# Which engine forms the low halves of 26 weight chunks: the mixer's convolution and narrow projections

## The chip, the cores and the metric

The kernel runs on one core of one Trainium2 chip. The metric is the device time in microseconds, the median over runs. A profiled execution carries the record of every engine: TensorE (PE, with its weight loads as PEld), VectorE (DVE), ScalarE (ACT), GpSimd (POOL) and SyncE (SP, which issues DMAs). Numbers such as L2278 are lines of the kernel.

## The reference

Two transformer blocks in float32 over 512 tokens of width 1024. The part that the change touches is the input projection of the first block's mixer, once for the 512 tokens (`mix_sublayer`) and once for the 256 tokens of a context sequence (`context_states`):

```
h = modulate(rms_norm(x, norm_pre), mod3[:, 0], mod3[:, 1])
u_f, z, xbc, dt_raw = split(h @ w_in, ...)        # 256, 768, 1792, 24 columns
xbc = silu(centred_dwconv(xbc, conv_w) + conv_b)
dt  = softplus(dt_raw + dt_bias)
...
h = modulate(rms_norm(ctx, norm_pre), ...)        # 256 context tokens
xb, dt_raw = split(h @ w_in[:, 1536:], ...)       # 1280, 24 columns
xb = silu(centred_dwconv(xb, conv_w[:, 512:]) + conv_b[512:])
dt = softplus(dt_raw + dt_bias)
```

A scan over states, a Fourier mixing, an output projection, a feed-forward layer and a whole second block follow.

## The kernel before, in words

Every large product is made with three TensorE passes in a reduced type. Each operand is held as a high half (its value rounded to that type) and a low half (value minus high half), and PE adds high x high, high x low and low x high (L1486 to L1488). Activations are split where they are made; weights are split as they arrive.

The weights come as one stream of chunks of up to 128 x 1024 numbers in the order in which PE uses them. For chunk j:

- SP loads it into one of three `raw` buffers. It waits until both halves of chunk j - 3 have been formed, which frees the buffer (`load`).
- ACT writes the high half into one of three `whi` buffers (L1837), when the load has landed and PE is through with chunk j - 3.
- DVE or GpSimd writes the low half, `raw - whi`, into one of three `wlo` buffers. DVE does it in one subtraction over the chunk (L2278), GpSimd in two over half the chunk each (L2776 and L2777). Both wait for the high half. PE waits for the low half when it begins the chunk.

The split of chunk c + 2 is placed at the step `begin` of chunk c, in each engine's program order. All engines run their own parts of one list of steps, in its order, so an operation that waits holds up all that is behind it on its engine.

Which engine forms the low half is decided by the name that a chunk carries in the stream: names in the tuple `LOW_BY_VECTOR` (L666) go to DVE, the first six chunks too, all others to GpSimd. `split` in `number` counts the events, and both engines' `w_low` follow that count. GpSimd does nothing else but one multiplication in each rotary embedding of the second block.

The steps around the change, in order of time:

- `ffn1c` (until 595 us): feed-forward layer over the context, low halves by DVE.
- `dt` (one chunk of 24 columns) and `xbc` (14 chunks, N = 512). For each output tile ACT evacuates PSUM with the middle tap of the convolution (L1916), DVE adds the outer taps (L2345, L2346, which read PSUM), ACT applies Silu (L2041), and six of the tiles are transposed by PE (L1567) one chunk later and copied by ACT (L2025). The rest of the context's feed-forward is woven between: DVE adds the norm's result (L2461, L2464), ACT squares (L1976), DVE sums the squares (L2431), PE reduces them over partitions (L1529), and then the pre-norm of the context is made in eight rounds that go from DVE (L2446) to ACT (L2000) and back to DVE (L2267), with two buffers. Then softplus (L2241 to L2257) and small products over `dt` (L1578).
- `cdt` (one chunk) and `cxb` (10 chunks, N = 256): the same for the context. Woven between are its softplus: DVE L2241, L2242, ACT L2047, DVE L2244, ACT L2049, DVE L2251 to L2257, L2488. Behind it PE makes twelve small products (L1598), ACT their exponentials (L2060), each in the engines' order.
- `uf`, `z`, `wo`: the other projections, with the scan beside them. Their low halves are formed by DVE before and after. From 921 us on GpSimd forms the low halves again.

PSUM has eight banks, six of which are handed round in turn to output tiles and small products.

Of the kernel before, what the change touches and what calls it, by code (L numbers as in the profile page):

```python
# [662 lines left out]
LN_EXP = "natural_log_exp_and_others"  # L663


LOW_BY_VECTOR = ("ffn1c", "dt", "xbc", "cdt", "cxb", "uf", "z", "wo")  # L666


SIGNALS = {
# [24 lines left out]
def number(S, stream):  # L694
# [3 lines left out]
    def mark(*event):  # L698
        sem = SEM_OF[event[0]]
        count[sem] = count.get(sem, 0) + 1  # L700
        assert event not in at, event
        at[event] = count[sem]
# [15 lines left out]
    def split(j):  # L718
        mark("hi", j)
        mark("lov" if stream[j][0] in LOW_BY_VECTOR or j < 2 * NS else "lop", j)  # L720

# [2139 lines left out]
```

## Time and profile before

| | |
|---|---|
| median of 3 runs | 3460.84 us (3460.06 to 3464.72) |
| the profiled execution | 3463.49 us, of which the span of the records is 3462.2 us |
| PE busy | 3381.9 us, 98% |
| DVE busy | 1610.9 us, 47% |
| ACT busy | 1418.3 us, 41% |
| GpSimd busy | 1321.3 us, 38% |
| granted TensorE clock, mean | 0.994 |
| chain that ended last | PE 87%, DVE 5%, ACT 3%, issue 2%, DMA 2%, POOL 1% |

Of the 40 slices of the span, GpSimd is idle in the six from about 433 to 910 us; in these the low halves are DVE's. The busy times say which engine has room. Whether a wait costs anything is seen in the waits of PE and in the chain that ended last, read for the stretch in question. A "duration" of DVE or GpSimd in these records runs from the start of the instruction and holds any time for which it is held up inside.

### The profile page before, as it was taken

How to read it: one execution, taken by the hardware profiler on the slowest of the kernel's cores; microseconds unless marked ns; L12 is line 12 of the kernel's file. 1: busy time of each engine (PE TensorE's matmuls, PEld its weight loads, DVE VectorE, ACT ScalarE, POOL GpSimd, SP SyncE). 2: the span in 40 equal slices, each digit the busy share in tenths (PEclk: the TensorE clock that was granted, in tenths of full speed). 3: DMA queues.
4: the chain of work that ended last, by engine and by line, in shares of the span. 5: the costliest groups of instructions: out<-in, count | busy, mean ns of one | idle time of the engine just before them, and what ended most of it. 6: DMA issues, size and time to landing. Idle time of an engine off the chain costs nothing.

```text
span 3462.2 us, 44383 instructions
## 1 busy us (share of the span) xinstructions
PE 3381.9 (98%) x16880; PEld 2716.5 (78%) x16880; DVE 1610.9 (47%) x3080; ACT 1418.3 (41%) x2397; POOL 1321.3 (38%) x1032
## 2 busy tenths in 40 slices
PE   7999999998999999999999999999999999999998
PEld 5888899885688887777776888887877776788887
DVE  6856566666520115755542343232865452344142
ACT  4223455654532224354443344343354453344242
POOL 2776200000044443434433444444534333444443
PEclk9999999999999999999999999999999999999999
DMA  7566455221123323223222222323323222223332
GB/s 305 201 217 218 128 185 170 87 88 49 49 91 92 104 86 103 89 68 98 80 91 73 91 92 89 101 89 115 100 74 95 79 75 92 91 80 96 99 96 87
DMA packets 117716, 373.26 MB, mean 108 GB/s; under 512 B 15360, under 2 KB 16256, under 8 KB 117120
## 3 DMA queue, kind: packets, MB, share of 16 engines
q1 hardware_dynamic: 115024, 364.74, 32.5%
q10 hardware_dynamic: 2480, 5.68, 0.5%
q8 instruction: 135, 2.21, 0.3%
q14 instruction: 77, 0.63, 0.1%
HBM read 356.73 MB, written 2.10 MB: 104 GB/s over the span
## 4 chain that ended last, share of the span: by engine, by line
PE 87%; DVE 5%; ACT 3%; issue 2%; DMA 2%; POOL 1%; SPq 1%; ACTq 0%; DVEq 0%; POOLq 0%
PE ps L1486 26%; PE ps L1488 25%; PE ps L1487 25%; PE ps L1756 2%; PE ps L1773 1%; PE ps L1738 1%; PE ps L1529 1%; ACT b L1837 1%; DVE b L2278 1%; PE ps L1733 1%; DVE b L2446 1%; PE ps L1546 1%; PE ps L1797 1%; PE ps L1808 1%; DMA b<-b 1%
## 5 line engine op out<-in xcount | busy, mean ns | idle before, releaser
L1486 PE MATMUL ps<-b,b 128*128 128x512 f32 (+1 forms) x4688 | 1768.5, 377 | 27.3 <-DVE b L2267 6.0
L1488 PE MATMUL ps<-b,b 128*128 128x512 f32 (+1 forms) x4688 | 1733.9, 370 | 0.0
L1487 PE MATMUL ps<-b,b 128*128 128x512 f32 (+1 forms) x4688 | 1732.5, 370 | 0.0
L2776 POOL TENSOR_TENSOR b<-b,b 128x512 fp32r<-128x512 f32 (+1 forms) x494 | 629.1, 1273 | 2082.3 <-ACT b L1837 2078.8
L1486 PEld LDWEIGHTS ps<-b,b 128*128 128x128 f32 x4688 | 883.9, 189 | 216.0 <-issue 52.2
L1488 PEld LDWEIGHTS ps<-b,b 128*128 128x128 f32 x4688 | 883.6, 188 | 153.7
L1487 PEld LDWEIGHTS ps<-b,b 128*128 128x128 f32 x4688 | 884.6, 189 | 148.5 <-issue 5.5
L1837 ACT ACTIVATE b<-b 128x1024 fp32r<-128x1024 f32 (+1 forms) x618 | 603.8, 978 | 318.7 <-PE ps L1488 306.5
L2777 POOL TENSOR_TENSOR b<-b,b 128x512 fp32r<-128x512 f32 (+1 forms) x494 | 650.0, 1316 | 0.0
L1901 ACT ACTIVATE b<-b 128x512 fp32r<-128x512 f32 (+1 forms) x110 | 64.8, 589 | 347.7 <-DVE b L2322 244.7
L2408 DVE CUSTOM_DVE_ANT_0 b<-b,b,b 128x1024 bf16<-128x1024 f32 x108 | 188.2, 1742 | 39.7 <-DMA b<-in_ada 32.2
L2313 DVE SCALAR_TENSOR_TENSOR b<-ps,b,b 128x511 f32<-128x511 f32 x88 | 66.0, 750 | 248.7 <-ACT b L1891 248.7
L2278 DVE TENSOR_TENSOR b<-b,b 128x1024 fp32r<-128x1024 f32 (+2 forms) x124 | 138.9, 1123 | 81.1 <-ACT b L1837 80.7
L2322 DVE TENSOR_TENSOR b<-ps,b 128x512 f32<-128x512 f32 (+1 forms) x66 | 39.6, 599 | 277.4 <-PE ps L1488 271.1
L2659 DVE CUSTOM_DVE_ANT_0 b<-ps,b 128x128 f32<-128x128 f32 (+2 forms) x192 | 87.2, 454 | 157.9 <-PE ps L1756 131.3
L2154 ACT ACTIVATE b<-b,b 128x128 f32<-128x128 f32 (+2 forms) x192 | 102.2, 534 | 97.0 <-DVE b L2666 68.7
L1976 ACT ACTIVATE b<-b 128x512 f32<-128x512 f32 (+1 forms) x112 | 64.2, 582 | 186.3 <-DVE b L2341 60.1
L2170 ACT ACTIVATE b<-ps 128x128 f32<-128x128 f32 (+2 forms) x192 | 69.0, 409 | 150.6 <-PE ps L1756 150.2
L1891 ACT ACTIVATE b<-ps,b 128x512 f32<-128x512 f32 x88 | 68.6, 779 | 97.1 <-PE ps L1488 96.8
L2336 DVE TENSOR_TENSOR b<-b,ps 128x512 f32<-128x512 f32 x32 | 22.0, 687 | 185.3 <-PE ps L1488 185.3
L2328 DVE TENSOR_TENSOR b<-b,b 128x512 fp32r<-128x512 f32 (+1 forms) x110 | 70.2, 638 | 80.8 <-ACT b L1901 80.8
L2677 DVE TENSOR_SCALAR b<-b,b 128x128 f32<-128x128 f32 (+2 forms) x192 | 100.9, 526 | 6.8
(240 smaller groups left out, 2378.6 us busy)
## 6 DMA issues: line engine op xcount, KB each, us to landing
b<-in_w SPq DMA_DIRECT2D x454, 512.0 KB, 3.4
b<-in_ada SPq DMA_DIRECT2D x86, 512.0 KB, 5.6
b<-in_w SPq DMA_DIRECT2D x80, 384.0 KB, 3.1
b<-in_w SPq DMA_DIRECT2D x80, 320.0 KB, 2.9
b<-b SPq DMA_DIRECT2D x160, 64.0 KB, 2.0
b<-in_const SPq DMA_DIRECT2D x24, 256.0 KB, 3.8
b<-in_x SPq DMA_DIRECT2D x2, 1024.0 KB, 11.3
out<-b SPq DMA_DIRECT2D x8, 256.0 KB, 2.0
```

What stands on the lines that cost most here:

```text
L1486: pe.matmul(out, a[0], b[0], start=first, stop=False, **kw)
L1487: pe.matmul(out, a[0], b[1], start=False, stop=False, **kw)
L1488: return pe.matmul(out, a[1], b[0], start=False, stop=last, **kw)
L1837: act.activation(whi[j % NS][:, 0:nk * w], raw[j % NR][:, 0:nk * w], ACT.Copy).then_inc(up("hi", j), 1)
L2154: m = act.activation(q[:, 0:hi - lo], q[:, 0:hi - lo], ACT.Exp, bias=sx[:, 1:2], accum_out=sx[:, 2:3])
L2278: dve.tensor_tensor(wlo[j % NS][:, 0:nk * w], raw[j % NR][:, 0:nk * w], whi[j % NS][:, 0:nk * w].bitcast(F32), ALU.subtract).then_inc(up(" ...
L2328: dve.tensor_tensor(hl[:, i % 11, 0:N], q[:, 0:N], hh[:, i % 11, 0:N].bitcast(F32), ALU.subtract).then_inc(up("hl", f, i), 1)
L2408: m = dve.tensor_tensor_reduce(spare[:, :], ada_slot(x)[:, :], cb[:, w, :], 1.0, pv("ada_b", p), ALU.mult, ALU.add, mod[:, p, w:w + 1])
L2659: dve.tensor_tensor_reduce(Lg[u % 6][:, 0:w], PB[st["bank"][p]][:, 0:w], mk, 0.125, -3e38, ALU.add, ALU.max, sx[:, 0:1]).then_inc(up("t1", ...
L2677: dve.tensor_scalar(q, q, sx[:, 4:5], None, ALU.mult).then_inc(up("pr", a, l, u), 1)
L2776: pool.tensor_tensor(wlo[j % NS][:, 0:h], raw[j % NR][:, 0:h], whi[j % NS][:, 0:h].bitcast(F32), ALU.subtract)
L2777: then(pool.tensor_tensor(wlo[j % NS][:, h:2 * h], raw[j % NR][:, h:2 * h], whi[j % NS][:, h:2 * h].bitcast(F32), ALU.subtract), "lop", j)
```

## The change

Four names leave the tuple, so that GpSimd forms the low halves of the chunks that carry them: `dt` (1), `xbc` (14), `cdt` (1) and `cxb` (10). GpSimd's two subtractions take the place of DVE's one for each. Nothing else changes: the loads, the high halves, the order of steps and the buffers are the same.

```
-LOW_BY_VECTOR = ("ffn1c", "dt", "xbc", "cdt", "cxb", "uf", "z", "wo")
+LOW_BY_VECTOR = ("ffn1c", "uf", "z", "wo")
```

## Rows read from the trace of the kernel before

**Rows 1.** Page, part 1: busy time, share of the span, instructions.
```profile
PE 3381.9 (98%) x16880; PEld 2716.5 (78%) x16880; DVE 1610.9 (47%) x3080; ACT 1418.3 (41%) x2397; POOL 1321.3 (38%) x1032
```

**Rows 2.** Windows: stretch, length, busy of each engine, granted clock, DMA share, GB/s.
```profile
700.00:720.00 20.00, 16.73 (x123) 16.32 (x122) 11.51 (x27) 14.77 (x27) 0.00 (x0) 0.83 0.41 132
```

**Rows 3.** Waits of PE, 592 to 745 us: total, times, longest.
```profile
PE ps L1486 <- DVE b L2346: 2.2, 1, 2.2
...
PE ps L1598 <- DVE b L2488: 1.0, 1, 1.0
```

**Rows 4.** Line L2278, 592 to 729 us: durations in ns, first and last start.
```profile
L2278 DVE TENSOR_TENSOR b<-b,b x26: 350/1216/1226, 592.8 to 725.1; 128x1024 fp32r<-128x1024 f32 x24, 128x192 fp32r<-128x192 f32 x2
```

**Rows 5.** Timeline, start and duration: one chunk's halves with DVE quiet.
```profile
925.46 1.05 ACT L1837 ACTIVATE b<-b 128x1024 fp32r<-128x1024 f32 x1
...
926.65 1.30 POOL L2776 TENSOR_TENSOR b<-b,b 128x512 fp32r<-128x512 f32 x1 [2.90 <-ACT b L1837]
927.90 1.29 POOL L2777 TENSOR_TENSOR b<-b,b 128x512 fp32r<-128x512 f32 x1
```

**Rows 6.** Timeline: another pre-norm of N = 256, with GpSimd at work.
```profile
356.53 0.98 POOL L2776 TENSOR_TENSOR b<-b,b 128x320 fp32r<-128x320 f32 x1 [0.44 <-ACT b L1837]
356.81 0.98 DVE L2446 SCALAR_TENSOR_TENSOR b<-b,b,b 128x256 f32<-128x256 f32 x1
357.47 1.06 POOL L2777 TENSOR_TENSOR b<-b,b 128x320 fp32r<-128x320 f32 x1
357.71 1.09 DVE L2267 SCALAR_TENSOR_TENSOR b<-b,b,b 128x256 fp32r<-128x256 f32 x1
...
361.05 0.48 DVE L2446 SCALAR_TENSOR_TENSOR b<-b,b,b 128x256 f32<-128x256 f32 x1
```

**Rows 7.** Timeline: a one-input DVE operation beside GpSimd and alone.
```profile
1494.46 1.30 POOL L2777 TENSOR_TENSOR b<-b,b 128x512 fp32r<-128x512 f32 x1
1494.49 1.48 DVE L2677 TENSOR_SCALAR b<-b,b 128x384 f32<-128x384 f32 x1
...
1496.09 0.42 DVE L2677 TENSOR_SCALAR b<-b,b 128x384 f32<-128x384 f32 x1
```

**Rows 8.** Timeline: the last sum of squares of the context's norm.
```profile
635.69 1.05 ACT L1837 ACTIVATE b<-b 128x1024 fp32r<-128x1024 f32 x1
637.93 0.71 ACT L1976 ACTIVATE b<-b 128x256 f32<-128x256 f32 x2
638.41 0.42 DVE L2431 TENSOR_TENSOR b<-b,b 128x256 f32<-128x256 f32 x1
638.88 0.70 PE L1529 MATMUL ps<-b,b 128*128 128x256 f32 x2 [1.19 <-DVE b L2431]
```

**Rows 9.** Timeline: three chunks with the context's pre-norm beside them.
```profile
655.61 0.77 ACT L1916 ACTIVATE b<-ps,b 128x512 f32<-128x512 f32 x1
...
668.87 0.77 ACT L1916 ACTIVATE b<-ps,b 128x512 f32<-128x512 f32 x1
...
671.24 0.63 ACT L2041 ACTIVATE b<-b 128x512 f32<-128x512 f32 x1 [0.65 <-DVE b L2346]
...
672.23 0.60 PE L1567 MATMUL ps<-b,b 128*128 128x128 f32 x4
```

**Rows 10.** Timeline: the high half of a context chunk.
```profile
704.57 1.06 ACT L1837 ACTIVATE b<-b 128x1024 fp32r<-128x1024 f32 x1
```

**Rows 11.** The chain that ended last, in order of time: start, duration, what.
```profile
705.78 1.13 DVE b L2278
...
707.31 0.22 DVE b L2252
...
708.77 0.28 DVE b L2488 x2
...
713.93 0.58 PE ps L1486
```

**Rows 12.** Windows, columns as in rows 2.
```profile
711.60:718.40 6.80, 4.58 (x22) 4.47 (x22) 2.25 (x4) 3.87 (x10) 0.00 (x0) 0.50 0.47 157
```

## The prediction, made before the changed kernel was built

> **What bounds the kernel now.** I read the page first, then the waits of PE and the chain that ended last over the stretch where the 26 chunks are split, and then the timelines of DVE, ACT and GpSimd side by side there. PE is busy for 98% of the span [rows 1], so a microsecond taken from DVE or given to GpSimd counts only where PE waits for it. From 592 to 745 us PE waits little: 1.19 us for the last sum of squares (L2431) [rows 8], 1.0 us for the end of the context's softplus (L2488), 2.2 us for a PSUM bank that L2346 frees [rows 3], and one wait in the scan of the initial states, which starts when the moved chunks are done. The last two are one chain. The chain that ended last runs there through DVE: the low half L2278 at 705.78, six softplus steps, L2488 at 708.77, ACT's and DVE's work on two tiles, and PE again at 713.93 [rows 11]. From 700 to 720 us PE is busy for 16.73 us of 20 at a mean clock of 0.83 [rows 2], and from 711.6 to 718.4 us the clock was 0.50, the lower of its two levels, 1.2 GHz, behind the wait for L2488 [rows 12]. So the stake is not DVE's busy time but when some ten short operations run.
>
> **What is removed.** DVE loses 24 subtractions of 1.22 us and two of 0.35 us, 24 x 1.218 + 0.7 = 29.9 us [rows 4]. Of this only what stands directly ahead of a waited-for operation is on a path: 1.13 us at 705.78 [rows 11], and next to nothing ahead of L2431. That one starts at 638.41, as the subtraction ends, but its square is done only at about 638.3, half-way through the pair at 637.93 [rows 8].
>
> **What is added.** GpSimd does a full chunk in two operations that end 2.54 us after the first starts (926.65 to 929.19), which is 0.14 us after the high half ends [rows 5]. That is 24 x 2.54 = 61 us on an engine that is idle in the whole stretch, and each low half is ready some 2.7 us after the high one, where a free DVE needs 1.3 us. PE needs it two chunks after the high half may be made. In `xbc` that is over 10 us. In `cxb` 22 matmuls at the lower clock are 4.58 us of PE [rows 12], 0.21 each, so some 0.11 at the full clock and 2.6 us a chunk of 24. Two chunks are 5.2 us, less 1.05 for the high half and 2.7: 1.5 us are left. Cost nothing; what covers it are these two chunks of PE work, and if ACT comes more than 1.5 us late the cover is gone, unless PE itself is waiting. The raw buffer is freed 1.4 us later, and its next load has a chunk's time more than it needs: nothing either. GpSimd has nothing else queued. DVE, ACT and SP get no new wait in their programs.
>
> **The cost that the diff does not show.** There is a pre-norm of the same shape with GpSimd at work [rows 6]. L2446, which reads two SBUF tensors, takes 0.48 us alone and 0.98 beside L2776, L2267 takes 1.09 beside L2777, and GpSimd's own operations stretch too (1.06 for 0.88). Each ends some 0.3 us after the other engine's operation does. So the two engines take turns, one whole instruction each. A DVE operation with one SBUF tensor of this kind, L2677, takes 0.42 alone and 1.48 beside GpSimd [rows 7]. Operations that read PSUM (L2345, L2346) show no such stretch where their kind runs beside GpSimd elsewhere in the trace. A chunk now holds DVE's SBUF operations off for up to 1.25 us twice, once for each half: 2.5 us for 1.22 freed. Whoever is second waits for the remainder, then GpSimd's second half goes ahead of DVE's next operation.
>
> GpSimd takes 2.54 us a chunk against 1.22 [rows 4, 5]. The Trainium skill (GPSIMD Engine Reference, section "When to use GPSIMD") says to leave two-input elementwise work to VectorE, as GpSimd is about twice as slow. The trace agrees on the ratio, 2.1. If all of that stood on PE's path, the sum would be + 24 x 1.3 = 32 us; by the waits of PE none of it does. The skill (SBUF — State Buffer, section "Who interferes with whom") makes the pair of ports that the two engines share an exclusive lock, taken for a whole instruction when DVE reads two SBUF tensors. The durations of 0.98 and 1.09 agree [rows 6]. If instead the two shared bandwidth, the terms below would be about half.
>
> **Term A, the sum of squares.** The high half ends at 636.74, so GpSimd works from 636.88 to 638.13 and to 639.4. L2431 wants to start at 638.35, inside the second half, and starts at 639.4 instead of 638.41: PE resumes 1.0 us later. Ends: 0 (the square is a little earlier and goes first) to 1.25.
>
> **Term B, the pre-norm.** DVE and ACT are slower than PE here: L1916 starts at 655.61 and 668.87, 6.63 us a chunk [rows 9], in one serial chain of evacuation, taps, low half and three rounds L2446, L2000, L2267. The low half leaves it (- 1.14). The first L2446 then meets GpSimd's first half, of which about 0.8 us remain, and the next DVE operation the second, 1.25. With the round trip to ACT behind each, the chunk gets 0.6 to 0.9 us longer. Three such chunks: + 2.3 us. The Silu L2041 ends at 671.87, and PE wants its result for L1567 at about 672.3 [rows 9], 0.4 to 0.5 us later. PE waits 1.8 us. Ends: 0 to 2.5.
>
> **Term C, the context's softplus.** The high half ends at 705.63 [rows 10], GpSimd works from 705.77. L2251 starts 1.05 us earlier than now, L2252 then waits for the first half (707.0) and L2253 for the second (708.5). The five steps behind it at 0.24 and L2488 end at 710.1 instead of 709.05: + 1.05. Ahead of that, L2242 and L2244 meet the chunk before in the same way, less what they gain: + 0.8, ends - 0.1 and 1.25. Both delays push the last steps into the next chunk's pair, which ACT's high half starts: none, one or two halves, 0 to 2.5, taken as 1.9, since the steps come 0.24 us apart and seldom slip through. Sum + 3.7. Behind it stand the same operations of ACT and DVE as now, so PE resumes at 713.93 + 3.7. Ends: - 0.9 to 5.
>
> **Term D, the clock.** PE idles longer around 710 us, so the twelve small products and the six matmuls behind them fall to 1.2 GHz too: six at 0.1 us more, and a tenth for the small ones, + 0.7. The matmuls from 713.93 on ran at that clock already. Ends: - 2.3 (no fall: half of the 4.58 us [rows 12]) to + 3.4 (a fall as long as that one, 6.8 us, once more).
>
> Everything later follows PE, so no slack takes this back: the next wait of PE, for the initial states, starts from the end of `cxb`, with low halves of `uf` and `z` still on DVE.
>
> **Sum.** 1.0 + 1.8 + 3.7 + 0.7 = + 7.2 us. Durations come from the profiled execution of 3463.49 us, 2.65 above the median; on that it would give 3470.7. On the median of 3460.84 it gives 3468.0.
>
> **Rivals.**
> - The turns cost less than they seem (GpSimd's halves fall into DVE's PSUM operations and idle time, and the pre-norm's lag stays inside its 0.4 us and the tiles' buffers). A 0.3, B 0.3, C 1.0: 3462.5. For it: DVE is busy for about two thirds only, and half of that with PSUM operands. Against it: the waits come right behind the high half, where the taps end too. Chance 0.20.
> - Faster: the mechanism is term C without blocks, and it decides from the point where the steps L2242 to L2257 lose less than 1.13 us in all. Then L2488 ends 1.05 earlier, the wait of 1.0 us is gone, and if that keeps the clock up, the 4.58 us of matmuls at 1.2 GHz become 2.3 [rows 12]. - 1.05 - 2.3: 3457.5. Against it: the stretched operations [rows 6, 7]. Chance 0.06.
> - Low halves late in `cxb`: the 1.5 us of cover go, since ACT is delayed by term C and GpSimd's own halves stretch, and two or three chunks start 1 to 2 us late; or the clock falls once more, behind terms A or B. + 4: 3472. Chance 0.15.
> - The 26 chunks do not move. The tuple is read only in `split`, and both `w_low` follow it, so they do: 0.01, 3460.8.
>
> The forecast has the rest, 0.58.
>
> **Range and chances.** The forecast's own range is 3464.5 to 3471. With the rivals the range is 3460.5 to 3474, which leaves out the faster one and a second fall of the clock on top of all. Within 0.2%, 6.9 us, is about what a measurement of this kernel can tell from no change; the forecast of + 7.2 sits on that edge. Slower by more: half of the forecast's 0.58 and a little, 0.32, and the late low halves, 0.15: 0.47. Within: 0.26 + 0.20 + 0.03 + 0.01 = 0.50. Faster by more than 6.9 us would take the whole of PE's waits here: 0.03.
>
> **What would show it.** Steps: L2446, L2267, L2464 and L2431 between 606 and 672 us with durations of 0.8 to 1.7 us in place of 0.42 to 0.48; GpSimd's operations from 1.29 to 1.7; a wait of PE for L2431 of about 2.2 us (A); a new wait of PE's transposes L1567 for L2041 near 673 to 675 us (B); L2488 about 3.7 us later against its chunk, and a wait of PE for it of some 5 us (C); the clock at 0.5 for longer than 6.8 us around 715 us (D); no wait of PE for L2777. It is wrong if those DVE operations keep their durations, or if they stretch and PE's waits stay as they are.

## The result, and the profile after

| | before | after |
|---|---|---|
| median, us | 3461.39 (3459.84 to 3466.14, 9 runs) | 3469.45 (3467.91 to 3471.66, 9 runs) |
| profiled run, us (span) | 3463.49 (3462.2) | 3469.81 (3468.5) |

The changed kernel takes 1.002 times as long, with a 95% interval of 1.0011 to 1.0029; the medians are 8.1 us apart. The forecast was 3468.0, + 7.2 us, with a range of 3460.5 to 3474. The time and its sign are right; of the four terms that made it up, one was right, one was nothing, one was twice too large, one was too small, and one cost was missing.

One thing has to be known ahead of every number below: the same kernel does not repeat to a microsecond. In 96 runs of the kernel before beside the experiments it took 3459.2 to 3468.2 us. They fall by their mean granted clock: 32 runs at 0.995 took 3459.2 to 3462.9, 38 runs at 0.993 took 3463.2 to 3468.2. So a wait of PE, read from one profile, says more than the time of one run, and ratios with their intervals more than medians.

The busy time after, page part 1, to be read beside [rows 1]:

```profile
PE 3384.5 (98%) x16880; PEld 2720.2 (78%) x16880; DVE 1603.0 (46%) x3054; ACT 1417.3 (41%) x2397; POOL 1383.1 (40%) x1084
```

26 subtractions have left DVE and 52 have come to GpSimd, so the chunks moved. GpSimd gained 61.8 us, as worked out. DVE should have lost 29.9 us and lost 7.9: the other 22 us are operations of DVE that now last longer, though they do the same work. That is the first sign of the mechanism.

The waits of PE from 592 to 760 us after (engine, what waited, on whom: total, times, longest), to be read beside [rows 3] and, for L1529, [rows 8]:

```profile
PE ps L1598 <- DVE b L2488: 3.0, 1, 3.0
PE ps L1608 <- issue: 2.6, 1, 2.6
PE ps L1529 <- DVE b L2431: 2.0, 1, 2.0
PE ps L1486 <- DVE b L2346: 2.0, 1, 2.0
...
PE ps L1578 <- issue: 0.5, 1, 0.5
```

Three are longer than before: L1598 for L2488 by 2.0, L1529 for L2431 by 0.8, and a new one at L1578. One is shorter, L1486 for L2346, by 0.25 us (1.97 in the timeline, 2.22 before). L1608 and its two waits are as before. There is no wait of L1567 for L2041, which term B of the prediction had asked for, and none for L2777.

**Where each wait comes from.** The timeline after, around the sum of squares, beside [rows 8]:

```profile
636.44 1.26 POOL L2777 TENSOR_TENSOR b<-b,b 128x512 fp32r<-128x512 f32 x1
636.69 1.30 DVE L2431 TENSOR_TENSOR b<-b,b 128x256 f32<-128x256 f32 x1 [1.00 <-ACT b L1976]
638.04 0.70 PE L1529 MATMUL ps<-b,b 128*128 128x256 f32 x2 [2.03 <-DVE b L2431]
```

L2431 takes 0.42 us alone [rows 8]. It starts 0.25 after GpSimd's second half, and ends 0.29 after it: 1.30. PE stands 0.84 us longer.

The timeline after, around the softplus of the context's time steps, beside [rows 11]:

```profile
704.59 1.29 POOL L2776 TENSOR_TENSOR b<-b,b 128x512 fp32r<-128x512 f32 x1 [0.62 <-ACT b L1837]
704.66 1.28 DVE L2242 TENSOR_TENSOR b<-b,b 128x48 f32<-128x48 f32 x1
705.00 1.28 ACT L2045 ACT_TABLE_LOAD   x1
...
709.27 1.29 POOL L2776 TENSOR_TENSOR b<-b,b 128x512 fp32r<-128x512 f32 x1 [2.14 <-ACT b L1837]
709.68 0.95 DVE L2252 TENSOR_TENSOR b<-b 128x48 f32<-128x48 f32 x1
710.53 1.28 POOL L2777 TENSOR_TENSOR b<-b,b 128x512 fp32r<-128x512 f32 x1
710.66 1.20 DVE L2253 TENSOR_TENSOR b<-b 128x48 f32<-128x48 f32 x1
711.90 0.21 DVE L2254 SCALAR_TENSOR_TENSOR b<-b 128x48 f32<-128x48 f32 x1
...
712.67 1.28 POOL L2776 TENSOR_TENSOR b<-b,b 128x512 fp32r<-128x512 f32 x1 [0.87 <-ACT b L1837]
712.87 1.22 DVE L2488 TENSOR_TENSOR b<-b,b 128x24 f32<-128x24 f32 x2
```

The row of L2254 shows what such a step takes alone, 0.21 us. L2252 meets the first half (0.95), and L2253 the second (1.20). The four steps behind them run freely, and L2488, 0.28 before, meets the first half of the next chunk (1.22). L2242 is held as well, but costs nothing: it ends at 705.94, and ACT loads its table until 706.28 anyway.

The new gap is at the context's decays, L2479, four products of 128x24. After, and then the same operation before:

```profile
682.15 1.29 POOL L2776 TENSOR_TENSOR b<-b,b 128x512 fp32r<-128x512 f32 x1 [2.92 <-ACT b L1837]
682.18 2.68 DVE L2479 TENSOR_TENSOR b<-b,b 128x24 f32<-128x24 f32 x4
683.40 1.33 POOL L2777 TENSOR_TENSOR b<-b,b 128x512 fp32r<-128x512 f32 x1
684.96 1.26 PE L1578 MATMUL ps<-b,b 128*128 128x12 f32 x10 [0.48 <-issue]
```

```profile
679.54 0.46 DVE L2479 TENSOR_TENSOR b<-b,b 128x24 f32<-128x24 f32 x4
```

Before, L2479 was done at 680.00, and PE came to L1578 at 683.58 without a wait. After, it is late by the lag of the pre-norm ahead of it, and so it falls on the low half of `cxb` 0, which holds it for 2.68 us in place of 0.46.

**Where the time came from.** The start of one and the same instruction of PE, from the timelines of before, of after, and of a second profile of the changed kernel (full_again, told below), in us. A step in the shift is time gained or lost there.

| instruction of PE | before | after | shift | full_again | shift |
|---|---|---|---|---|---|
| L1553 | 607.08 | 605.41 | -1.67 | 605.92 | -1.16 |
| L1529, behind L2431 | 638.88 | 638.04 | -0.84 | 638.55 | -0.33 |
| L1567, first | 642.19 | 642.93 | +0.74 | 641.86 | -0.33 |
| L1567, sixth | 672.23 | 672.97 | +0.74 | 671.90 | -0.33 |
| L1578 | 683.58 | 684.96 | +1.38 | 683.90 | +0.32 |
| L1580 | 687.07 | 690.11 | +3.04 | 687.47 | +0.40 |
| L1598, behind L2488 | 709.19 | 714.24 | +5.05 | 711.55 | +2.36 |
| L1567, after it | 711.33 | 718.21 | +6.88 | 715.07 | +3.74 |
| L1567 | 718.87 | 725.33 | +6.46 | 722.68 | +3.81 |

At 607 us the two profiles of the changed kernel are 1.67 and 1.16 us ahead, which is no effect of the change: no chunk is moved before 592 us, and from 592 to 607 PE is busy for the whole 15 us in all three profiles. From there to the last line they lose 8.1 and 5.0 us. The waits are the same in both: 0.83 at L1529, 0.64 and 0.65 at L1578, 1.97 and 1.96 at L1598, together 3.4 us, less the 0.25 us by which the wait of L1486 for L2346 got shorter. The rest is the clock: 4.9 us in one profile, 1.8 in the other.

The windows of after show where (stretch, length, busy time and count of PE, PEld, DVE, ACT, POOL, granted clock, DMA share, GB/s), and then those of full_again:

```profile
639.00:642.40 3.40, 3.40 (x9) 2.64 (x9) 0.00 (x0) 0.00 (x0) 0.00 (x0) 0.50 0.37 146
687.00:694.00 7.00, 7.00 (x36) 6.16 (x36) 2.43 (x6) 5.92 (x8) 1.71 (x2) 0.53 0.10 41
714.00:724.20 10.20, 8.00 (x36) 7.63 (x37) 2.05 (x6) 5.58 (x11) 3.73 (x3) 0.51 0.22 74
```

```profile
639.00:642.40 3.40, 3.40 (x19) 2.81 (x18) 0.00 (x0) 0.00 (x0) 0.00 (x0) 1.00 0.55 154
687.00:694.00 7.00, 7.00 (x48) 6.06 (x48) 2.44 (x6) 6.16 (x9) 2.77 (x3) 0.76 0.04 8
714.50:721.30 6.80, 4.84 (x23) 4.43 (x23) 1.08 (x3) 3.48 (x5) 2.51 (x2) 0.50 0.16 57
```

Behind the same wait of 2.03 us for L2431, PE ran 3.4 us at 1.2 GHz (0.50) in one profile, and at 2.4 GHz (1.00) in the other. Behind the wait for L2488 the lower clock lasts 10.2 us in one, and 6.8 in the other, as long as before [rows 12].

### The profile page after: what moved, and what is told of

It is laid out like the page before. It is cut to its first block, busy times and chain, and to the rows that moved or that the text cites. A ratio compares the mean times of both kernels' runs of the same rounds, so it can differ in the third digit from the quotient of the medians.

```text
span 3468.5 us, 44435 instructions
## 1 busy us (share of the span) xinstructions
PE 3384.5 (98%) x16880; PEld 2720.2 (78%) x16880; DVE 1603.0 (46%) x3054; ACT 1417.3 (41%) x2397; POOL 1383.1 (40%) x1084
## 4 chain that ended last, share of the span: by engine, by line
PE 87%; DVE 5%; ACT 3%; DMA 1%; issue 1%; POOL 1%; SPq 1%; ACTq 0%; POOLq 0%; DVEq 0%
PE ps L1486 26%; PE ps L1488 26%; PE ps L1487 25%; PE ps L1756 2%; PE ps L1773 1%; PE ps L1738 1%; PE ps L1529 1%; DMA b<-b 1%; PE ps L1733 1%; ACT b L1837 1%; PE ps L1546 1%; PE ps L1797 1%; PE ps L1808 1%; DVE b L2446 1%; SPq L1417 1%
## 5 line engine op out<-in xcount | busy, mean ns | idle before, releaser
L1486 PE MATMUL ps<-b,b 128*128 128x512 f32 (+1 forms) x4688 | 1768.7, 377 | 27.1 <-DVE b L2267 6.7
L2776 POOL TENSOR_TENSOR b<-b,b 128x512 fp32r<-128x512 f32 (+2 forms) x520 | 659.5, 1268 | 2026.6 <-ACT b L1837 2023.1
L1486 PEld LDWEIGHTS ps<-b,b 128*128 128x128 f32 x4688 | 884.5, 189 | 215.0 <-issue 52.7
L2777 POOL TENSOR_TENSOR b<-b,b 128x512 fp32r<-128x512 f32 (+2 forms) x520 | 682.8, 1313 | 0.0
L2278 DVE TENSOR_TENSOR b<-b,b 128x1024 fp32r<-128x1024 f32 (+1 forms) x98 | 108.7, 1115 | 71.7 <-ACT b L1837 71.6
```

Source lines behind the costliest of these rows:

```text
L1486: pe.matmul(out, a[0], b[0], start=first, stop=False, **kw)
L2278: dve.tensor_tensor(wlo[j % NS][:, 0:nk * w], raw[j % NR][:, 0:nk * w], whi[j % NS][:, 0:nk * w].bitcast(F32), ALU.subtract).then_inc(up(" ...
L2776: pool.tensor_tensor(wlo[j % NS][:, 0:h], raw[j % NR][:, 0:h], whi[j % NS][:, 0:h].bitcast(F32), ALU.subtract)
L2777: then(pool.tensor_tensor(wlo[j % NS][:, h:2 * h], raw[j % NR][:, h:2 * h], whi[j % NS][:, h:2 * h].bitcast(F32), ALU.subtract), "lop", j)
```

## Experiments

The theory after the two traces: a DVE operation that reads SBUF waits, once it meets a subtraction of GpSimd, until that whole instruction ends, and this costs only where PE waits for the DVE operation. That is at five chunks of the 26: `xbc` 8 (for L2431), `cxb` 0 (for L2479) and `cxb` 4 to 6 (for the softplus and L2488). The rivals: the lag that the other chunks put on the pre-norm and on the buffers costs as much, or the lower clock alone does.

**One name group at a time.** GpSimd forms the low halves of `dt` and `xbc` alone:

```diff
-LOW_BY_VECTOR = ("ffn1c", "dt", "xbc", "cdt", "cxb", "uf", "z", "wo")
+LOW_BY_VECTOR = ("ffn1c", "cdt", "cxb", "uf", "z", "wo")
```

> The change for dt and xbc alone (15 chunks); cdt and cxb stay with VectorE. The trace of the full change shows four places where PE loses time: the sum of squares (+ 0.84 us of wait, then 1.6 us at the lower clock), the small products over dt (+ 0.5 us of wait, 1.8 at the lower clock), the context's softplus (+ 2.0 us) and the products behind it (+ 1.2 us). Theory, that blocked operations on VectorE's waited-for chains cause all of it: only the sum of squares remains, + 2.4 us; the products over dt are late only when the lag of the pre-norm and GpSimd's work on the first cxb chunk come together, so they cost nothing here. Rival, that the cost goes with the number of chunks that GpSimd forms: 15 of 26, + 4.6 us. The sum over L2446 and L2267 stretches to 1.2 to 1.5 us in the pre-norm by the first theory, without a new wait of PE for L1567.

And those of `cdt` and `cxb` alone:

```diff
-LOW_BY_VECTOR = ("ffn1c", "dt", "xbc", "cdt", "cxb", "uf", "z", "wo")
+LOW_BY_VECTOR = ("ffn1c", "dt", "xbc", "uf", "z", "wo")
```

> The change for cdt and cxb alone (11 chunks); dt and xbc stay with VectorE. Theory: only the context's softplus and the products behind it are late, + 3.2 us; the products over dt are not, since VectorE's pre-norm has no lag. So this run and the one with xbc alone should add up to 5.6 us, 2.3 less than the whole change. Rival, cost by number of chunks: + 3.4 us here, and the two add up to the whole, 8. The two rivals part in the sum and in whether PE waits ahead of L1578.

Measured: xbc_only 1.0003 (0.9994 to 1.0012), cxb_only 1.0009 (1.0000 to 1.0018) of the kernel before. The waits of PE in the two profiles, xbc_only first:

```profile
PE ps L1529 <- DVE b L2431: 2.0, 1, 2.0
...
PE ps L1598 <- DVE b L2488: 1.0, 1, 1.0
```

```profile
PE ps L1598 <- DVE b L2488: 3.0, 1, 3.0
...
PE ps L1529 <- DVE b L2431: 1.2, 1, 1.2
```

The waits divide as the theory says: each group carries its own and leaves the other's as it was. Neither profile has the gap at L1578, which needs both: the lag of `xbc` and the low half of `cxb` 0. As times, the ratios are + 1.0 us (-2.1 to +4.2) and + 3.1 us (0 to +6), beside forecasts of 2.4 and 3.2. The rival, cost by number of chunks, had + 4.6 and + 3.4: the first lies just outside its interval, the second can't be told from the forecast. It is the waits that speak here.

**Five chunks, and the other 21.** The edit for five, in the plan of the split; the other kernel moves all but these:

```diff
+FIVE = (("xbc", 8), ("cxb", 0), ("cxb", 4), ("cxb", 5), ("cxb", 6))
...
-        mark("lov" if stream[j][0] in LOW_BY_VECTOR or j < 2 * NS else "lop", j)
+        key = stream[j][0]
+        nth = j - next(x for x in range(len(stream)) if stream[x][0] == key)
+        mark("lov" if (key in LOW_BY_VECTOR and (key, nth) not in FIVE) or j < 2 * NS else "lop", j)
```

> Only five of the 26 chunks go to GpSimd, those whose formation overlaps the waited-for operations: xbc 8, cxb 0, 4, 5 and 6. Theory: the sum of squares costs its 2.4 us and the softplus with what is behind it 3.2, + 5.6 us in all; the products over dt nothing, as the pre-norm has no lag. Rival, cost by number: 5 of 26, + 1.5 us.

> The full change without those five chunks: GpSimd forms 21, VectorE xbc 8 and cxb 0, 4, 5 and 6. Theory: every waited-for operation is as free as before, 0 us (within 1 us), though VectorE's pre-norm still lags by some 2 us and its operations there are blocked as much as in the full change. Rival, cost by number: 21 of 26, + 6.5 us. If the lag of the pre-norm cost PE anything, as term B of the prediction had it, + 1.8 us.

Measured: five_only 1.0017 (1.0009 to 1.0026), all_but_five 0.9999 (0.9990 to 1.0008). The waits of PE for the same operations, whose line numbers are four higher in these two files, five_only first:

```profile
PE ps L1602 <- DVE b L2492: 3.0, 1, 3.0
...
PE ps L1533 <- DVE b L2435: 2.0, 1, 2.0
```

```profile
PE ps L1533 <- DVE b L2435: 1.2, 1, 1.2
...
PE ps L1602 <- DVE b L2492: 1.0, 1, 1.0
```

This settles the place. Five chunks cost what 26 cost, to within the intervals: + 5.9 us (3.1 to 9.0), where cost by number asked for + 1.5. The other 21, some 50 us of GpSimd's time, cost nothing that shows: - 0.3 us (-3.5 to +2.8), where cost by number asked for + 6.5. The lag of the pre-norm is in this run, 7.23 us a chunk by the starts of L1916 at 653.62 and 668.08 (L1920 in this file), in place of 6.63. Term B of the prediction (+1.8 from the pre-norm) lies inside the interval of the time, but not in the profile: from the first L1567 to L1578 PE takes 41.40 us (639.88 to 681.28), and took 41.39 before (642.19 to 683.58).

**GpSimd writes, but reads nothing.** In the changed kernel, GpSimd's subtractions of the 26 chunks become writes of zero of the same tiles in four pieces; the low halves of these chunks are thereby left out of the result.

```diff
+                if STREAM[j][0] in ("dt", "xbc", "cdt", "cxb"):
+                    for x in range(0, 2 * h, h // 2):
+                        p = pool.memset(wlo[j % NS][:, x:x + h // 2].bitcast(F32), 0.0)
+                    then(p, "lop", j)
+                    return
```

> The full change, but for the 26 chunks GpSimd only writes: it fills the low half with zeros in four pieces instead of subtracting, so the low halves of these weights are left out of the result. VectorE has lost its 26 subtractions as in the full change. Theory, that GpSimd's reads of SBUF are what holds VectorE's operations with two SBUF operands off: L2446, L2267, L2431 and L2252 go back to their short durations (0.48, 0.48, 0.42, 0.21 us) although GpSimd still works beside them; the wait for L2431 is that of before, 1.2 us, L2488 comes 1.0 us earlier than in the kernel before, and its wait of 1.0 us is gone: 1 to 3 us faster than before. Rival, that any GpSimd instruction blocks them: they stretch, by less since a piece is short, and the waits stay above those of before. A third theory, that a cost lies in the longer way of the low half to PE, would make this faster too, but would leave the durations stretched.

Measured: 1.0000 (0.9991 to 1.0008). The timeline of write_only around the softplus:

```profile
703.98 1.07 POOL L2778 MEMSET b<- 128x256 f32 x4 [3.19 <-ACT b L1837]
704.41 0.21 DVE L2252 TENSOR_TENSOR b<-b 128x48 f32<-128x48 f32 x1
704.66 0.21 DVE L2253 TENSOR_TENSOR b<-b 128x48 f32<-128x48 f32 x1
```

GpSimd is at work for 1.07 us beside these steps, and none is stretched: 0.21 each. The shortness of the pieces doesn't explain this, for eighths of a subtraction, told below, stretch the same steps to 0.39. So it is GpSimd's reading of SBUF that holds DVE, and not its work as such. The Trainium skill (SBUF — State Buffer, section "Who interferes with whom") says that a DVE instruction with two SBUF inputs contends with a GpSimd instruction that reads SBUF, and not with one that only writes it. These rows agree.

The run says something more. Here all 26 subtractions are gone from DVE and nothing is held, and the wait for L2488 is gone altogether. In the profile PE gets through this stretch 1.3 us sooner than before: from the second L1567 ahead of the wait for L2346 to the second behind it, 703.86 to 719.78, where before it took from 705.62 to 722.85. The lower clock still comes behind that wait, though for a shorter time (0.53 from 712.3 to 715.6 us). A gain of 1.3 us is smaller than the time can show, whose interval is -3.1 to +2.8 us, so the forecast of 1 to 3 us is neither shown nor refuted. That bounds what such relief of DVE can bring in this place: 3 us at most.

**Is it the waits, or the clock?** In the changed kernel, 12 and 8 matmuls whose result nothing reads fill the waits for L2488 and for the first matmul of `cxb` 5.

```diff
+        def fill(c, count):
+            at.wait_ge(*n("hi", c))
+            b, w = bank_of(6), whi[c % NS]
+            for _ in range(count):
+                pe.matmul(b[:, :], w[:, 0:128], w[:, 0:512], start=True, stop=True)
...
+                if c == BASE["cxb"] + 5 and x == 0:
+                    at.wait_ge(*n(*lo_event(c)))
+                    fill(c, 8)
...
+                if i == 0 and d == 0:
+                    fill(BASE["cxb"] + 4, 12)
```

> The full change, with matmuls that nothing uses in the two long waits of PE: twelve of N = 512 ahead of L1598 (2.7 us in a wait of 3.0) and eight ahead of the first matmul of cxb 5 (1.8 us in a wait of 2.0). They add nothing to the result. Theory of term D, that idle time of PE brings the lower clock: from L1598 on PE stays at 2.4 GHz, L1598 with its six matmuls takes 1.8 us less and the matmuls of cxb 5 some 2 us less, so 3 to 4 us faster than the full change, + 4 to + 5 over before. Rival, that the clock falls there for another reason (the small products themselves): no gain, + 8.

Measured: 1.0019 (1.0010 to 1.0028), 3464.8 to 3474.0 us. A window of its profiled run, columns as above:

```profile
714.00:724.20 10.20, 9.78 (x80) 9.27 (x79) 3.69 (x8) 6.60 (x11) 5.06 (x4) 1.00 0.20 72
```

The waits are full (0.2 and 0.4 us are left of 3.0 and 2.0), the clock stays at 2.4 GHz, and that run, at 3464.8, is the fastest of the eleven. The other ten are not faster than the changed kernel. So with the waits filled the fall of the clock near 715 us can be absent, but this does not bring the kernel back to the time of before. What the clock did in those ten runs was not recorded by stretch. The mean granted clock of each run is known: seven of the ten had 0.995 and took 3466.8 to 3471.3 us, where the kernel before took 3462.9 at most with that mean. So a low mean clock is not what holds these runs back, and the fills do not give back what the change costs; why the ten are slower than the profiled one stays open.

**The other side: the kernel before, with L2488 earlier.** If L2488 came 1.1 us earlier in the kernel before, would it gain? VectorE forms the low half of `cxb` 5 after L2488 in place of before it:

```diff
-                    w_low(st["c"] + 2)
+                    if st["c"] + 2 != BASE["cxb"] + 5:
+                        w_low(st["c"] + 2)
...
                     p.then_inc(up("cda"), 1)
+                    w_low(BASE["cxb"] + 5)
```

> The kernel before, with one operation moved: VectorE forms the low half of cxb 5 after L2488 instead of ahead of the softplus steps L2251 to L2488. All 26 chunks are VectorE's. This takes the 1.13 us off the chain without GpSimd. Theory: L2488 comes 1.1 us earlier, PE's wait for it goes from 1.0 us to 0, L2346 and the restart of PE come 0.9 us earlier, - 0.9 us, and up to 2.3 more if the clock stays up. Rival, that the chain is held by ACT's table loads there: no change.

And the same, with 9 unused matmuls ahead of the first one of `cxb` 5:

> The kernel before with that later low half and nine unused matmuls (2.0 us) in the wait ahead of cxb 5. Theory: - 0.9 us as in the run without them, and the matmuls of cxb 5 at 2.4 GHz, - 2 us more: about - 3 us against before. Rival: the small products L1598 alone bring the clock down, then - 0.9 us only.

Measured: 1.0003 (0.9994 to 1.0012) and 1.0002 (0.9993 to 1.0010). No gain shows. The - 0.9 us forecast for the first lies inside its interval (-2.1 to +4.2 us), so the time can't refute it; the - 3 us forecast for the second lies outside its own (-2.4 to +3.5). The timeline of before_later_low says why (L2347 is L2346 in this file, L2489 is L2488):

```profile
706.48 0.28 DVE L2489 TENSOR_TENSOR b<-b,b 128x24 f32<-128x24 f32 x2
706.67 1.22 DVE L2278 TENSOR_TENSOR b<-b,b 128x1024 fp32r<-128x1024 f32 x1
...
706.90 1.03 PE L1598 MATMUL ps<-b,b 128*128 128x12 f32 x8
...
708.32 0.48 DVE L2347 SCALAR_TENSOR_TENSOR b<-ps,b,b 128x255 f32<-128x255 f32 x1
...
708.86 0.61 PE L1598 MATMUL ps<-b,b 128*128 128x12 f32 x4 [0.93 <-DVE b L2347]
```

The wait for L2488 is gone, and the first eight matmuls of L1598 run freely. But the subtraction now stands between L2488 and the next tile's outer taps, which before followed L2488 at once (708.96, where L2488 starts at 708.77 [rows 11]). The last four matmuls need the PSUM bank that L2347 frees, and wait 0.93 us for it, in place of the 1.04 us that L1598 waited for L2488. The 1.13 us were not taken off the chain but moved one step along it. So these two runs do not show what an earlier L2488 alone would bring; write_only does. In later_low_filled the nine matmuls themselves ran at the lower clock (0.52 from 709.9 to 713.4 us): they took 3.6 us in place of 2.0, and only what stood behind them ran at 2.4 GHz.

**The size of the pieces.** This is the run that tests the mechanism itself. The changed kernel, with GpSimd's subtraction of a chunk in one, four and eight instructions in place of two (`q` = 2h, h / 2 and h / 4):

```diff
-                pool.tensor_tensor(wlo[j % NS][:, 0:h], raw[j % NR][:, 0:h], whi[j % NS][:, 0:h].bitcast(F32), ALU.subtract)
-                then(pool.tensor_tensor(wlo[j % NS][:, h:2 * h], raw[j % NR][:, h:2 * h],
-                                        whi[j % NS][:, h:2 * h].bitcast(F32), ALU.subtract), "lop", j)
+                q = h // 4 if STREAM[j][0] in ("dt", "xbc", "cdt", "cxb") else h
+                for x in range(0, 2 * h, q):
+                    p = pool.tensor_tensor(wlo[j % NS][:, x:x + q], raw[j % NR][:, x:x + q],
+                                           whi[j % NS][:, x:x + q].bitcast(F32), ALU.subtract)
+                then(p, "lop", j)
```

> The full change, but GpSimd forms the low half of each of the 26 chunks in one subtraction of 128x1024 instead of two of 128x512. Two theories of a block. By 'one block per GpSimd instruction' (a dependent VectorE operation that starts beside a GpSimd subtraction ends with it, and the next gets in as soon as that one is over) the two operations L2252 and L2253 and the sum of squares L2488 at cxb 5 lose one long block in place of three short ones: the GpSimd instruction lasts some 2.5 us from 709.3 to 711.8, L2252 ends near 711.8, L2253 and L2488 follow at 0.21 and 0.42, done at about 712.5 instead of 714.1, ahead of the next chunk's subtraction at 712.7; the wait of the cxb 5 matmul falls from 3.0 to about 1.4. The wait for L2431 stays at 2.0, since it is the end of the chunk, not its middle, that releases it. Sum: -1.6 against the full change, a ratio of about 1.0015. By 'the block is mere contention, in proportion to the time shared' nothing changes: 3.0 and 2.0 again, ratio 1.002.

> The full change, but in four subtractions of 128x256, about 0.65 us each, per chunk. By 'one block per GpSimd instruction' each of L2252, L2253 and L2488 loses 0.6 instead of 1.2: L2488 is done some 1.8 earlier or more, and the wait of the cxb 5 matmul falls to about 1.0, where L2346 limits it; L2431 gets in one quarter earlier, its wait falls from 2.0 to about 1.4. Sum: -2.6, ratio about 1.001. By 'contention in proportion' both waits stay at 3.0 and 2.0, ratio 1.002 or a little above for the added instructions.

> The full change, but in eight subtractions of 128x128, about 0.35 us each, per chunk. By 'one block per GpSimd instruction' the waits are those of before plus at most 0.3: 1.0 and 1.2 to 1.4, and the time is that of the kernel before (ratio 1.000 to 1.001), with some 0.1 us per chunk of GpSimd time added by the further instructions, which nothing waits for. By 'contention in proportion' 3.0 and 2.0, ratio 1.002.

> The changed kernel itself once more, beside the other three on the same chip, to tell its waits and its lower-clock stretches apart. If the waits are its lasting cost and the clock steps behind them partly chance, the waits return to within 0.05 us (2.0, 3.0 and the issue gap of 0.5 at L1578) and the ratio is between 1.001 and 1.003, with the stretches at the lower clock at other places than in its first profile. If the lower clock behind the wait for L2431 is a fixed consequence, it stands at 638.9 again, the step of +1.6 with it.

All four ran beside the same 30 runs of the kernel before (median 3464.92). The duration of a piece is the mean from the groups of instructions from 592 to 760 us.

| kernel | a piece, us | wait for L2431 | gap at L1578 | wait for L2488 | ratio (95%) |
|---|---|---|---|---|---|
| one_piece | 2.39 | 1.9 | 0.7 | 4.7 | 1.0026 (1.0015 to 1.0036) |
| full_again (two) | 1.32 | 2.0 | 0.5 | 3.0 | 1.0018 (1.0009 to 1.0027) |
| four_pieces | 0.78 | 1.6 | none | 2.0 | 1.0003 (0.9994 to 1.0012) |
| eight_pieces | 0.50 | 1.2 | none | 1.3 | 0.9994 (0.9985 to 1.0003) |
| before | none | 1.2 | none | 1.0 | 1 |

The timeline of one_piece:

```profile
710.85 2.37 POOL L2778 TENSOR_TENSOR b<-b,b 128x1024 fp32r<-128x1024 f32 x1 [2.66 <-ACT b L1837]
711.26 2.03 DVE L2252 TENSOR_TENSOR b<-b 128x48 f32<-128x48 f32 x1
713.33 0.21 DVE L2253 TENSOR_TENSOR b<-b 128x48 f32<-128x48 f32 x1
...
714.25 2.34 POOL L2778 TENSOR_TENSOR b<-b,b 128x1024 fp32r<-128x1024 f32 x1 [1.03 <-ACT b L1837]
714.30 2.35 DVE L2257 SCALAR_TENSOR_TENSOR b<-b,b 128x48 f32<-128x48 f32 x1
716.69 0.28 DVE L2488 TENSOR_TENSOR b<-b,b 128x24 f32<-128x24 f32 x2
```

And of eight_pieces:

```profile
703.37 3.97 POOL L2778 TENSOR_TENSOR b<-b,b 128x128 fp32r<-128x128 f32 x9 [0.50 <-ACT b L1837]
...
704.40 0.39 DVE L2254 SCALAR_TENSOR_TENSOR b<-b 128x48 f32<-128x48 f32 x1
704.82 0.39 DVE L2255 TENSOR_TENSOR b<-b 128x48 f32<-128x48 f32 x1
```

A step of 0.21 us takes 2.03 or 2.35 us beside one piece, 0.95 or 1.20 beside a half, and 0.39 beside an eighth: it ends with the instruction that it met. By mere sharing of bandwidth it would not depend on how the same subtraction is cut. So the block is one whole GpSimd instruction, and the wait for L2488 and the time both go with its length. (The wait for L2431 does not grow from two pieces to one: the end of the chunk's subtraction is what frees it in both, as forecast.)

The wait for L2488 can be added up from the timelines. What the held steps lose against their free durations, less the 1.13 us of the subtraction that left DVE, is what the wait grows by. (L2244 counts where it is held, and L2242 only by what it outlasts ACT's table load.)

| kernel | lost by held steps, us | their sum less 1.13, us | growth of the wait from 1.04, us |
|---|---|---|---|
| one_piece | 1.82 + 2.14, and 0.81 by L2242 | 3.64 | 3.64 |
| full_again (two) | 0.74 + 0.99 + 0.94, and 0.42 by L2244 | 1.96 | 1.96 |
| four_pieces | 0.18 + 0.45 + 0.46 + 0.44 + 0.53 | 0.93 | 0.94 |
| eight_pieces | 0.14 + 0.18 + 0.18 + 0.18 + 0.17 + 0.49 | 0.21 | 0.21 |

The forecast for one_piece was wrong in sign (1.6 us less wait for L2488, where it grew by 1.7). It let L2488 follow L2253 at once and left out the four steps between them, L2254 to L2257, 0.24 us each. L2252 was released 2.4 us after its piece had begun, as forecast, but L2257 then came up at 714.30, 0.05 us after the next chunk's piece: two blocks that cost 1.8 and 2.1 us in place of three of 0.7 to 1.0. It also left out L2242: held for 2.40 us by one piece, it outlasts ACT's table load, and ACT's L2047 waits 0.81 us for it. The forecast for four_pieces had the wait for L2488 at about 1.0, and it was 2.0: with shorter pieces five steps met a piece, in place of three.

eight_pieces is the best form of the change: the same work on GpSimd, and no slower than before. It is not shown to be faster either, since its interval takes in 1, as does that of write_only. No kernel here is shown to beat the one before.

## Why the prediction came out right, point by point

- **What bounds the kernel.** Right. PE's waits carried the result: 22 us of stretched work on DVE cost only where PE waits for it.
- **What is added, and its cover.** GpSimd's busy time rose by 61.8 us for 61 forecast, no matmul waits for L2777, and no chunk is late. Right.
- **The cost that the diff does not show.** Right, and for the reason given: whole instructions in turn, read from [rows 6, 7]. It was then argued only; the pieces show it.
- **Term A (+1.0).** The wait grew by 0.83. Right, the size a little over. What it left to a rival, "the clock falls once more, behind terms A or B", happened in the first profile of the changed kernel (1.58 us), and not in its second.
- **Term B (+1.8).** Wrong: 0. The lag is there, and about as large as forecast: the L1916 that starts at 674.41 before starts at 677.32 after, and PE itself is 0.74 later there, so 2.2 us for 2.3. The rows of after, beside [rows 9]:

```profile
663.89 0.77 ACT L1916 ACTIVATE b<-ps,b 128x512 f32<-128x512 f32 x1
...
671.12 0.77 ACT L1916 ACTIVATE b<-ps,b 128x512 f32<-128x512 f32 x1
...
672.97 0.60 PE L1567 MATMUL ps<-b,b 128*128 128x128 f32 x4
673.49 0.63 ACT L2041 ACTIVATE b<-b 128x512 f32<-128x512 f32 x1 [0.66 <-DVE b L2346]
```

  A chunk takes 7.23 us in place of 6.63. But L1567 starts at 672.97, before the L2041 that it was said to need even begins at 673.49. The failed step is the reading of that pair. PE transposes the tile of the chunk before, not of the chunk just evacuated, so the transposes had a further period, some 6 us, and not 0.4. The description of the kernel above says so itself ("one chunk later"). Two rows that stand close in time were taken for a dependency; the wait list of before, which has no wait of L1567 for L2041, did not bear it out.
- **The missing term.** The same lag pushed L2479 onto the low half of `cxb` 0: 0.65 us in both profiles, and once 1.66 more by the lower clock. The prediction followed the lag to L1567 and stopped there. It should have followed it to the next operation of DVE that PE waits for.
- **Term C (+3.7).** The mechanism was right, the size was 1.96. Against its own three parts: at L2253 the net loss was 0.6 for 1.05, of which 0.3 is a miscount, for four steps and not five stand between L2253 and L2488 (L2254 to L2257, [rows 11] and the timeline above), and its own 708.5 leads to 709.8; ahead of the chunk's high half 0.4 for 0.8, since L2242's block ended under ACT's table load; and the next chunk's pair caught only L2488, one half and 0.95 for 1.9. The wait that it named, some 5 us for L2488, was 3.0.
- **Term D (+0.7).** Undersized, and not a constant: near L1598 it was 1.7 in both profiles, and the clock's whole share was 4.9 us in one and 1.8 in the other.
- **The sum.** 1.0 + 1.8 + 3.7 + 0.7 = 7.2 stands against 0.8 + 0.65 + 2.0 - 0.25 of waits and 1.8 to 4.9 of clock, 5.0 to 8.1. The total was right in part by luck: 3.5 us too much in B and C stood in for the clock and L2479.
- **The rivals.** "The turns cost less" put A, B and C at 1.6 in all, and they were 2.8. "Faster without blocks" is what write_only built: the wait for L2488 went, 1.3 us were gained in that stretch of its profile, and the lower clock came all the same, so its price of 3.3 us, which took the clock to stay up, was too high. The chances had faster at 0.03, which the result bears out.

## What to carry to other kernels

Where a DVE operation and a GpSimd operation both read SBUF, add to each short DVE operation on the path one whole GpSimd instruction, and count how many of a dependent chain start inside one; then cut the GpSimd work into short pieces. Eighths of 0.50 us took away all of this change's cost that could be measured. Work moved off a busy engine brings nothing where no other engine waits for it. An operation that is moved out from ahead of one waited-for operation must not land ahead of the next: look at what follows on the same engine, as PE may wait for that too. And follow a lag past the first consumer that has slack, to the next one that has none.

## What the runs showed of the hardware that was not expected

- What is held, and what is not. Beside a GpSimd subtraction, steps of 128x48 and 128x24 are held until it ends, just as large ones are, and L2244, a TENSOR_SCALAR with one SBUF tensor, too (0.61 for 0.19). L2251, a RECIPROCAL with one SBUF tensor, is not: it started 0.07 us ahead of the subtraction at 709.27 and kept its 0.44, and that subtraction kept its 1.29. So neither held the other; that L2251 came first is not shown to be the reason. Nor is one whose wide input is in PSUM: in one_piece L2345 took 0.47 us at 702.66, all of it beside a subtraction from 702.62 to 705.02. Nor were the steps beside a GpSimd write of zeros.
- The lower clock behind a wait is not a fixed consequence of its length: behind 2.03 us at the same place it came in one profile and not in the next. So its share of a small change can't be read from one profile. The spread of one kernel over 9 us goes with the mean granted clock; that the clock alone makes it is not shown.
- Cutting the subtraction costs GpSimd time: eight pieces of 0.50 us are 4.0 us a chunk in place of 2.6, on an engine that has it to spare here.
